# A two-layer hybrid decoder trunk: setup rebuilt, and x updated ahead of the slab splits

## The reference

```python
def rms_norm(x, g):
    y = x * rsqrt(mean(x * x, axis=-1) + 1e-6); return y * g

c_act = silu(c)                                    # c: (1, 1024)
for l in range(2):
    mod = c_act @ ada_w[l] + ada_b[l]              # (1, 9 * 1024)
    sh1, sc1, g1, sh2, sc2, g2, sh3, sc3, g3 = split(mod, 9)
    h = rms_norm(x, ffn1_norm[l]) * (1 + sc1) + sh1
    x = x + 0.5 * g1 * swiglu(h, ffn1_w_in[l], ffn1_w_out[l])       # FFN width 2816
    h = rms_norm(x, mix_norm[l]) * (1 + sc2) + sh2
    q, k, v, u, gates = split(h @ w_mix_in[l])
    lam = exp(sum(lq1 * lk1)) - exp(sum(lq2 * lk2)) + lam_init
    # 8 heads, two causal softmax maps each; bias[h, i, j] = rel_bias[h, bucket(i - j)]
    o = (softmax(q1 k1 / 8 + bias) - lam * softmax(q2 k2 / 8 + bias)) @ v
    o = rms_norm(o, subln_gain[l]) * (1 - lam_init)
    y_conv = silu(layer_norm(depthwise_conv31(a * sigmoid(g)))) @ w_conv_branch[l]
    merged = sigmoid(ga) * (o @ w_attn_branch[l]) + sigmoid(gb) * y_conv
    x = x + g2 * (merged @ w_mix_out[l])
    h = rms_norm(x, ffn2_norm[l]) * (1 + sc3) + sh3
    x = x + 0.5 * g3 * swiglu(h, ffn2_w_in[l], ffn2_w_out[l])
return rms_norm(x, final_norm)                     # x: (1, 512, 1024), float32
```

## Time and profile before

| | |
|---|---|
| median of 3 runs | 2756.42 us (2755.35 to 2757.57) |
| the profiled execution's own time, its span | 2755.38 us, 2753.7 us |
| mean granted clock of TensorE | 0.978 of full speed |
| PE busy | 2585.2 us (94%) |
| VectorE busy | 1748.2 us (63%) |
| ScalarE busy | 1060.4 us (39%) |
| POOL busy | 81.7 us (3%) |
| first layer matmul starts at | 83.1 us |

### The profile page before, as it was taken

The page is one execution under the profiler, slowest core; times in us unless marked ns, Lnnn a source line. Parts: engine busy times, 40 slices in busy tenths (PEclk is TensorE's granted clock), DMA queues, the critical chain, the costliest instruction groups (busy, mean ns, idle before and its releaser), DMA issues.

```text
span 2753.7 us, 35127 instructions
## 1 busy us (share of the span) xinstructions
PE 2585.2 (94%) x11186; PEld 2030.9 (74%) x11186; DVE 1748.2 (63%) x2545; ACT 1060.4 (39%) x1497; POOL 81.7 (3%) x162
## 2 busy tenths in 40 slices
PE   4899998999999989999979999989999999899997
PEld 2688886776767767888858888867766678688886
DVE  3655567799998555543345556669999965655433
ACT  2433322444443434343234342244444443443422
POOL 0000010000000000000000001100000000000000
PEclk9999998999999999999989999989999999999998
DMA  5444474222222233433324446622222223343332
GB/s 221 142 149 142 151 224 142 81 76 72 80 80 84 84 114 115 152 122 95 97 83 145 153 129 208 211 66 79 76 73 83 77 87 122 101 143 107 97 92 93
DMA packets 472262, 320.39 MB, mean 116 GB/s; under 512 B 11303, under 2 KB 447785, under 8 KB 471176
## 3 DMA queue, kind: packets, MB, share of 16 engines
q1 hardware_dynamic: 445260, 227.69, 28.1%
q0 software_dynamic: 21888, 83.90, 8.9%
q10 hardware_dynamic: 5052, 8.02, 1.0%
HBM read 314.52 MB, written 5.05 MB: 116 GB/s over the span
## 4 chain that ended last, share of the span: by engine, by line
PE 68%; DVE 16%; issue 11%; ACT 3%; ACTq 1%; DVEq 1%
PE bank L1045 21%; PE bank L1047 21%; PE bank L1046 21%; DVE conv_part L858 5%; DVE rstd L616 3%; DVE w_lo L605 2%; ACTq L420 1%; ACT w_hi L377 1%; DVE probs L890 1%; PE bank L1063 1%; PE bank L1064 1%; PE bank L1065 1%; PE bank L1100 1%; DVE probs L906 1%; PE bank L1127 1%
## 5 line engine op out<-in xcount | busy, mean ns | idle before, releaser
L605 DVE TENSOR_TENSOR w_lo<-w_raw,w_hi 128x1024 fp32r<-128x1024 f32 (+1 forms) x434 | 522.6, 1205 | 721.5 <-ACT w_hi L377 720.6
L1046 PE MATMUL bank<-h_lo,w_hi 128*128 128x512 f32 x2336 | 911.3, 390 | 0.0
L1045 PE MATMUL bank<-h_hi,w_hi 128*128 128x512 f32 x2208 | 885.9, 401 | 17.9 <-DVE w_lo L605 17.8
L1047 PE MATMUL bank<-h_hi,w_lo 128*128 128x512 f32 x2208 | 862.9, 391 | 0.0
L377 ACT ACTIVATE w_hi<-w_raw 128x1024 fp32r<-128x1024 f32 (+1 forms) x434 | 452.4, 1043 | 912.8 <-PE bank L1047 893.1
L1045 PEld LDWEIGHTS bank<-h_hi,w_hi 128*128 128x128 f32 x2208 | 415.5, 188 | 134.9 <-issue 52.2
L1046 PEld LDWEIGHTS bank<-h_lo,w_hi 128*128 128x128 f32 x2336 | 440.1, 188 | 89.9 <-issue 3.8
L1047 PEld LDWEIGHTS bank<-h_hi,w_lo 128*128 128x128 f32 x2208 | 415.4, 188 | 89.0
L858 DVE SCALAR_TENSOR_TENSOR conv_part<-glu,conv_taps,conv_part 128x512 f32<-128x512 f32 x464 | 316.6, 747 | 0.0
L1045 PE MATMUL bank<-s_hi,w_hi 128*128 128x512 f32 x704 | 274.9, 390 | 0.0
L1047 PE MATMUL bank<-s_hi,w_lo 128*128 128x512 f32 x704 | 274.0, 389 | 0.0
(11 more groups left out here) (158 smaller groups left out, 2296.5 us busy)
## 6 DMA issues: line engine op xcount, KB each, us to landing
w_raw<-in_ffn_w_in SPq DMA_DIRECT2D x176, 512.0 KB, 3.8
ada_raw<-in_ada_w POOLq DMA_DIRECT2D x144, 512.0 KB, 4.7
w_raw<-in_w_mix_in SPq DMA_DIRECT2D x112, 512.0 KB, 3.7
w_raw<-in_ffn_w_out SPq DMA_DIRECT2D x64, 512.0 KB, 3.6
w_raw<-in_ffn_w_out SPq DMA_DIRECT2D x32, 384.0 KB, 3.1
w_raw<-in_w_mix_out SPq DMA_DIRECT2D x18, 512.0 KB, 3.6
ada_first<-in_ada_w POOLq DMA_DIRECT2D x8, 1024.0 KB, 24.4
w_raw<-in_w_attn_branch SPq DMA_DIRECT2D x16, 512.0 KB, 3.6
```

The costliest lines, as they stand in the source:

```text
L605: dve.tensor_tensor(wlo[slot][:, 0:n, :], raw[slot][:, 0:n, :], whi[slot][:, 0:n, :].bitcast(F32), ALU.subtract).then_inc(w_lo[slot], 1)
L1045: pe.matmul(acc, wh, hi[:, k0 + k, :], start=first and k == 0, stop=False)
L1046: pe.matmul(acc, wh, lo[:, k0 + k, :], start=False, stop=False)
L1047: mm = pe.matmul(acc, wl, hi[:, k0 + k, :], start=False, stop=last and k == n - 1)
```

## The change

Setup. The bias rows of all heads come from one pair of matmuls (8 partitions, one per head), VectorE copies them out, and POOL's queue stores each row 128 times, reading one partition (nine stores as before, after the last ada_first load has landed); POOL waits for all of them, loads the first bias tile and goes on with ada_w. Lambda is loaded as rows of one partition and spread by a small matmul. The ada_first loads wait for the second x tile. x is transposed through four banks in place of two. Of the first modulation product VectorE does tiles 0, 1, 3, 5 and 7, and PE multiplies tiles 2, 4 and 6 as stationary operand by one column of c; PE also adds VectorE's sum, 16 columns, in the same place. Mean, root and reciprocal of the first norm stand inside that work.

Stages. In ffn_out and mo the update of x and its square stand ahead of the split of the next slab. The norm of the next layer (and the final one) stands at the end of the loop's round in place of its beginning.

```diff
+ADA0_PE = (2, 4, 6)
+ADA0_DVE = (0, 1, 3, 5, 7)
+ADA0_COL = 2 * KT + DEPTH
...
-    BR = [at(f"bias_row{i}", [P, TOK + P], F32, h0 + (8 if i < 3 else 24) * KB + 2560 * (i % 3)) for i in range(6)]
...
+    def bias_tile_rows(h):
+
+        src = BD[ds(h, 1), :]
+        return bass.AP(src.tensor, src.offset + (P - 1), [[TOK + P - 1, P], [1, TOK]])
...
+        pool.wait_ge(sem("x_in1"), 16)
...
-        pool.wait_ge(sem("ada0_step"), KT)
-        pool.wait_ge(sem("lam_dots"), 2 * DEPTH)
-        pool.wait_ge(sem("br_ready"), HEADS)
+        pool.wait_ge(sem("br_copied"), 2)
+        pool.wait_ge(sem(f"ada0_in{KT - 1}"), 16)
+        for row in range(HEADS + 1):
+            h = row % HEADS
+            pool.dma_start(BD[row, :].rearrange("(o p x) -> o p x", o=1, p=P),
+                           BR[h:h + 1, :].unsqueeze(1).to_broadcast([1, P, TOK + P])).then_inc(sem("br_out"), 16)
+        pool.wait_ge(sem("br_out"), 16 * (HEADS + 1))
+        pool.dma_start(BT[:, :], bias_tile_rows(0)).then_inc(sem("bt_first"), 16)
...
+        for n, name in enumerate(("lambda_q1", "lambda_k1", "lambda_q2", "lambda_k2")):
+            act.dma_start(LV[0:1, n, :, :], a[name].rearrange("(o l) d -> o l d", o=1)).then_inc(sem("lambda_in"), 16)
         for l in range(DEPTH):
             act.dma_start(CWR[0:CK, l, :], a["conv_dw"][l, :, :]).then_inc(sem("taps_in"), 16)
-        act.dma_start(TBR[0:HEADS, :], a["rel_bias"]).then_inc(sem("table_in"), 16)
-        act.dma_start(OH[0:BUCKETS + 1, :], onehot).then_inc(sem("table_in"), 16)
-        for l in range(DEPTH):
-            for n, name in enumerate(("lambda_q1", "lambda_k1", "lambda_q2", "lambda_k2")):
-                act.dma_start(LV[:, l, n, :], bass.AP(a[name].tensor, l * HD, [[0, P], [1, HD]]))\
-                    .then_inc(sem("lambda_in"), 16)
...
-        for h in range(HEADS):
-            act.wait_ge(sem("br_ready"), h + 1)
-            if h >= len(BR):
-                act.wait_ge(sem(f"br_out{h % len(BR)}"), 16)
-            if h == len(BR):
-                act.wait_ge(sem("br_again"), 16)
-            act.activation(BR[h % len(BR)][:, 0:TOK], ROW_BANKS[h % 2][0][:, :], ACT.Copy).then_inc(sem("br_part"), 1)
-            act.activation(BR[h % len(BR)][:, TOK:TOK + P], ROW_BANKS[h % 2][1][:, 0:P], ACT.Copy).then_inc(sem("br_copied"), 1)
-            act.wait_ge(sem("br_copied"), h + 1)
-            act.wait_ge(sem("br_part"), h + 1)
-            act.dma_start(BD[h, :].rearrange("(p x) -> p x", p=P), BR[h % len(BR)][:, :]).then_inc(sem(f"br_out{h % len(BR)}"), 16)
-            if h == 0:
-
-                act.dma_start(BD[HEADS, :].rearrange("(p x) -> p x", p=P), BR[0][:, :]).then_inc(sem("br_again"), 16)
...
+        root(0, 0)
...
+                        if m % 3 == 2:
+                            square_x(l * USES + USE0[n_out] + i, m // 3, (l * 3 + 1 + 2 * w) * KT, i * 2 + m // 3)
                         w_hi_part(l * PAIRS + PAIR0[n_out] + i * 3 + m // 2 + 1, m % 2,
                                   OUTG[(m + 2) % 3] if m < 4 else 8)
-                        if m % 3 == 2:
-                            square_x(l * USES + USE0[n_out] + i, m // 3, (l * 3 + 1 + 2 * w) * KT, i * 2 + m // 3)
                 if w == 1:
+
...
+                    root((l + 1) * AUXN, (l + 1) * UNITS)
...
+                        square_x(l * USES + USE0["mo"] + i, t, (l * 3 + 2) * KT, i * 2 + t)
                         w_hi_part(l * PAIRS + PAIR0["mo"] + i + 1, t)
-                        square_x(l * USES + USE0["mo"] + i, t, (l * 3 + 2) * KT, i * 2 + t)
...
+        def ada0_step(n, c0=0, c1=2 * D):
+
+            k = ADA0_DVE[n]
+            acc = ACC0[:, c0:c1]
+            dve.wait_ge(sem(f"ada0_in{k}"), 16)
+            if n == 0:
+                dve.wait_ge(sem("ca_ready"), 1)
+                ins = dve.tensor_scalar(acc, ADA0[:, k, c0:c1], CA[:, k:k + 1], None, ALU.mult)
+            else:
+                dve.wait_ge(sem("ada0_step"), n)
+                ins = dve.scalar_tensor_tensor(out=acc, in0=ADA0[:, k, c0:c1], scalar=CA[:, k:k + 1], in1=acc,
+                                               op0=ALU.mult, op1=ALU.add)
+            ins.then_inc(sem("ada0_step"), 1)
...
+        ada0_step(2)
+        reciprocal(0, 0)
+        ada0_step(3)
+        ada0_step(4, 0, D)
+        ada0_step(4, D, 2 * D)
+        for s in range(2):
+            w_lo_part(0, s)
+        dve.wait_ge(sem("lam_ready"), 1 + DEPTH)
+        dve.wait_ge(sem("mod_turned"), 1)
...
+                        if m % 3 == 2:
+                            t = m // 3
+                            update_x(p, m % 2, l * USES + USE0[n_out] + i, t, 2 * w, i * 2 + t)
+                        if w == 0:
                             for k in OUT_STEPS[m][:1]:
                                 ada_step(seq, k)
+                        if m % 3 == 2:
+                            sum_cleared(l * ZEROS + 1 + (ZERO_FFN2 if w else ZERO_FFN1))
+                            add_square((l * 3 + 1 + 2 * w) * KT, i * 2 + t)
...
+                    reciprocal((l + 1) * AUXN, (l + 1) * RSN)
...
-        def mod_sum(turn, src, rows):
-
-            pe.wait_ge(sem("modc_ready"), turn)
-            for r in range(rows):
-                mm = pe.matmul(O[0:64, :], SEL[:, ROWS_MAX - 1 - r:ROWS_MAX - 1 - r + 64],
-                               src[:, r * TOK:(r + 1) * TOK], start=(r == 0), stop=(r == rows - 1))
-            mm.then_inc(sem("mod_summed"), 1)
...
+        pe.wait_ge(sem("tb_rows"), 2)
+        pe.matmul(G[0][0:HEADS, :], TB[0:BUCKETS + 1, :], OH[0:BUCKETS + 1, 0:TOK], start=True, stop=True)
+        pe.matmul(G[1][0:HEADS, 0:P], TB[0:BUCKETS + 1, :], OH[0:BUCKETS + 1, TOK:TOK + P], start=True, stop=True)\
+            .then_inc(sem("br_ready"), 1)
...
+        pe.wait_ge(sem("lam_ready"), 1)
+        zeros = SEL[:, ROWS_MAX:ROWS_MAX + 2 * KT]
+        ones = SEL[:, ROWS_MAX - 1:ROWS_MAX]
+        pe.matmul(O[:, ADA0_COL:ADA0_COL + 2 * KT], ident[:, :], zeros, start=True, stop=False).then_inc(sem("mod_summed"), 1)
+
+        def ada0_columns(src, column, c0=0, c1=2 * KT, last=False):
+            for c in range(c0, c1):
+                mm = pe.matmul(O[:, ADA0_COL + c:ADA0_COL + c + 1], src[:, c * P:(c + 1) * P], column,
+                               start=False, stop=last and c == 2 * KT - 1)
+            return mm
+
+        pe.wait_ge(sem("ca_ready"), 1)
+        for n, k in enumerate(ADA0_PE):
+            pe.wait_ge(sem(f"ada0_in{k}"), 16)
+            ada0_columns(ADA0[:, k, :], CA[:, k:k + 1])
+            if n == 0:
+                norm_mean(0, KT)
+        for half in range(2):
+            pe.wait_ge(sem("ada0_step"), len(ADA0_DVE) + half)
+            mm = ada0_columns(ACC0, ones, half * KT, (half + 1) * KT, True)
+        mm.then_inc(sem("mod_turned"), 1)
...
+                    norm_mean((l + 1) * AUXN, ((l + 1) * 3 + 1) * KT)
```

More of the change, by code:

```diff
@@ L398, in norm_units @@
         def norm_units(l, k):
-            root(l * AUXN + AUX_NORM[k], l * UNITS + UNIT_NORM[k])
+            if k:
+                root(l * AUXN + AUX_NORM[k], l * UNITS + UNIT_NORM[k])
             act.wait_ge(sem("ac_ready"), l * 3 + (k + 1))
@@ L427, in _ @@
             act.wait_ge(sem("xp_ready"), j + 1)
-            act.activation(X[:, j, :], bank[2 + j % 2][:, :], ACT.Copy).then_inc(sem("x_ready"), 1)
-            act.wait_ge(sem("ssum_add"), j)
-            act.activation(SQ[:, :], bank[2 + j % 2][:, :], ACT.Square).then_inc(sem("sq_ready"), 1)
+            act.activation(X[:, j, :], bank[2 + j % 4][:, :], ACT.Copy).then_inc(sem("x_ready"), 1)
+            if j >= 4:
+                act.wait_ge(sem("ssum_add"), j - 3)
+            act.activation(SQ4[j % 4][:, :], bank[2 + j % 4][:, :], ACT.Square).then_inc(sem("sq_ready"), 1)
         act.wait_ge(sem("tapsp_ready"), DEPTH)
@@ L644, in norm_units @@
         def norm_units(l, k):
-            reciprocal(l * AUXN + AUX_NORM[k], l * RSN + RS_NORM[k])
+            if k:
+                reciprocal(l * AUXN + AUX_NORM[k], l * RSN + RS_NORM[k])
             u = l * UNITS + UNIT_NORM[k]
@@ L747, in _ @@
             lam_init = 0.8 - 0.6 * math.exp(-0.3 * l)
-            dve.scalar_tensor_tensor(out=nlam[:, l:l + 1], in0=lam_exp[:, 2 * l + 1:2 * l + 2], scalar=lam_init,
-                                     in1=lam_exp[:, 2 * l:2 * l + 1], op0=ALU.subtract, op1=ALU.subtract)\
-                .then_inc(sem("lam_ready"), 1)
+            dve.scalar_tensor_tensor(out=lam_row[0:1, l:l + 1], in0=lam_exp[0:1, 2 * l + 1:2 * l + 2], scalar=lam_init,
+                                     in1=lam_exp[0:1, 2 * l:2 * l + 1], op0=ALU.subtract, op1=ALU.subtract)\
+                .then_inc(sem("lam_rows"), 1)
@@ new lines, in _ @@
+        for j in range(4):
+            add_first_square(j)
+        ada0_step(0)
+        for j in range(4, KT):
+            add_first_square(j)
+        ada0_step(1)
+        dve.wait_ge(sem("lam_wide"), 1)
```

(36 more changed lines are left out.)

85 lines of the change are left out of this document (33 added, 52 removed).

## The result

The changed kernel takes 2799.6 us (median of 4 runs) against 2757.0 us before, measured beside it: ratio 1.0156, 95% interval 1.014 to 1.0172. It is slower by 1.6%; the forecast was 2804. Its profiled execution has a span of 2799.0 us, 45.3 us over the 2753.7 before.

A forecast was written before the change was run, and what follows sets the result against it. The prediction took PE matmul time (68% of the chain) as the bound, with losses only where PE stands still. It summed 2755.4 + 58.7 (second slab pair) - 10.3 (stage ends, layer step) = 2803.8 us; 8-in-10 range 2717 to 2816.

The forecast's parts named there:

- The stores: Setup: nine bias stores, each reading one partition, get one engine's 26.5 GB/s, take 111 us and land at 153.7.
- From the stores' end to the second pair: Setup: after w_hi 1.06 and w_lo 1.23, PE starts the second slab pair at 156.1, not 97.4: +58.7 us.
- Slabs share packet by packet: Setup DMA: a slab advances one packet per store packet on shared engines, so the second pair lands at 153.7.
- The two bounds of the stall: PE's setup wait once stores are slow: +54 us by the ada_w tile behind POOL's wait, +59 with slabs held.
- Stage ends: Five stage ends where a norm is recomputed: x ahead of the split gains 2.2 us each, -11.1 in all.
- case 4: Stage ends: ScalarE's later split costs what the earlier square gains, +11 us, so 2815 or 2734; chance 0.1.
- The step to layer 2: Layer 1 to 2: VectorE's jump back now follows the reciprocal, +0.75 us, bounds -2.2 and +2.
- The setup: Before the first layer matmul: narrow passes at 0.13 us, first matmul at 61.2, 21.9 us earlier.
- case 2: Stores not slow, so the setup gain of 21.9 us and the stage ends count: 2723 us; chance 0.36.
- Where the sign turns: Bias stores over 66 us make the kernel slower, under 55 us faster by more than the noise.

The follow-up runs named there:

- g4: Changed kernel with POOL waiting for each bias store before the next and the first chunk's eight ada_w tiles sent ahead or between stores: 2773.7 us, ratio 1.0061.
- f3: Kernel before the change with only the order altered, x updated and squared ahead of the slab splits: 2742.2 us, ratio 0.9948.
- f1: Changed kernel with each bias store reading two neighbouring partitions, 2h and 2h + 1, 64 rows from each: 2733.5 us, ratio 0.9917.
- f6: As e4, with POOL's wait for the stores and the first bias tile also moved behind its first three chunks of ada_w: 2807.9 us, ratio 1.0187.
- g1: Changed kernel with each bias store cut into two transfers of 64 rows, from partition h and from h + 64: 2754.1 us, ratio 0.9993.
- e1: Changed kernel with each bias store reading two partitions, h and h + 32, 64 rows from each: 2759.5 us, ratio 1.0015.
- e2: Changed kernel with each bias store reading two partitions, h and h + 64, 64 rows from each: 2734.6 us, ratio 0.9926.
- e4: Changed kernel with the bias stores, source unchanged, issued from ScalarE's queue instead of POOL's: 2806.8 us, ratio 1.0188.

## Why the prediction was right, and where not

- **The number** (2804 forecast, 2799.6 measured) is closer than its terms. The stores' end was forecast 10.2 us too late, which is too much in the sum; left out or too small were 3.0 us between the stores and the second pair, 2.6 of the clock and some 1.6 elsewhere.
- **The stores** (right, a tenth too slow). One partition fed 29.2 GB/s over the phase, forecast 26.5: they ended at 143.5, not 153.7. Spreading the source took 64.6 us off the time (2799.6 to 2735.0), which shows the cause. The 26.5 was one engine's share; in the trace all 16 engines are busy with the stores (95.8% of their time from 60 to 100 us) and it is the source that gives no more. Why the two rates are alike no run here shows.
- **From the stores' end to the second pair** (mis-sized). Forecast 2.4 us, measured 5.4: a table load of 1.28 and the tile's own gate steps stood there too. With the stores 10.2 earlier this makes +51.5 for +58.7. The clock's 2.6 us behind the idle stretch were not in the sum.
- **Slabs share packet by packet** (wrong, though the landing came out). The step drawn from the earlier trace rows failed: between 60 and 100 us the stores' queue moved 282 packets and the slabs', asked for from 57.8 us on, none. From 110 to 130 it was 143 and 160, packet by packet after all, and from 135 to 142 it was 66 and 846. The forecast also took the stores' packets for 2560 B; the large ones carried 5120.

```profile
q0 software_dynamic: 282, 1.17, 95.8%
```
```profile
q0 software_dynamic: 66, 0.25, 45.0%
q1 hardware_dynamic: 846, 0.43, 20.2%
```

  Slabs were not slowed in proportion from the start but held first. It ended at the stores' end either way, so the landing at 144.4 is no evidence for the step. g4 shows the hold, and its price with one store queued: 17.6 us.
- **The two bounds of the stall,** +54 by POOL's wait alone and +59 by the slabs. The slab came first (144.4; the ada_w tiles were issued at 144.61). POOL's wait by itself was not measured in the changed kernel; in g4 it held TensorE for 18.2 us.
- **Stage ends** (right). 10.5 us for 11.1, and f3 alone confirms it; case 4 falls. The step to layer 2 cost 0.95 for 0.75, with the spread said above. The 0.6 at the very end I had not priced; that three other profiles with the same code (f1, f6, g1) lack it speaks against a fixed cost of the moved reciprocal.
- **The setup** (case 2's size was wrong). The taps landed at 35.8 (forecast 35.5), but 128 narrow passes took 0.213 in place of 0.13 us: 128 x 0.083 = 10.6 us, and the first matmul came 10.2 later than 61.2. The value came from the earlier trace rows, passes in a stretch at 2.4 GHz; these ran at 1.2. With fast stores the change gives 2735, not 2723.
- **Where the sign turns** (about right). I put it at stores of 55 to 66 us. 69.9 us gave 1.0015 and 47.7 us 0.9917, but 54.0 us, which should have been faster beyond the noise, gave 0.9993.

## What to carry to other kernels

Before a broadcast replaces a store, ask how many partitions all transfers in flight read together, and how far apart these lie (h and h + 64 gave 103 GB/s where h and h + 32 gave 54); spread the source over the partitions, even when the values are the same. A slow transfer costs most through what waits behind it: look for the loads of the main loop that are asked for while it runs, and for the engine that waits for it before it issues its next loads. Take the price of a TensorE instruction from a stretch whose granted clock is the one that it will run at.

## What the runs showed of the hardware

- One-column matmuls back to back, TensorE busy 26.00 of 26.00 us, leave the granted clock at 0.50 (36 to 62 us of the changed kernel); a pass takes 0.213 us there.
- Before the first record of a trace the clock column prints 1.00, whatever the passes say: 0.50 by their pace in the kernel before up to 69.3 us.
- Stores that read one partition got 27 GB/s over 50 to 60 us, and others 54, 103 or 244 by which partitions were read together. Stores with 2 as outer dimension ran side by side (e1, e2, f1), those with 128 copies of one row landed behind each other.
- Nine broadcast stores held ScalarE in its issues for 81.4 us on its own queue (e4); on POOL's the same nine took 4.66 us to issue.
- A slab asked for at 57.8 us behind nine slow stores got no packet through between 60 and 100 us. With one store queued at a time (g4) slabs landed up to 13.0 us after their issue, median 8.4.
